# A hybrid attention and expert step on one core: rows turned early, three first units together, last norms scaled last

## The reference, cut to what matters

```
mod = silu(cond) @ w_ada + b_ada          # shift, scale, gate, twice; one set per kind of token
h   = ln_plain(x) * (1 + sc1) + sh1
q,k,v | bq,bk,bv | gates = h @ w_in       # w_in is 1024 x 6656
mix = attention of two kinds, gated;  x = ln_affine(ALPHA*x + g1*(mix @ w_o))
h   = ln_plain(x) * (1 + sc2) + sh2
y   = two of 16 experts per token, weighted and summed
out = ln_affine(ALPHA*x + g2*y, ln2_g, ln2_b)   # mean, variance, gain, bias over 1024
```

## Time and profile before

| what | us |
|---|---|
| median of 3 runs | 1408.13 (1407.26 to 1408.39) |
| the profiled execution's own time | 1407.71 |
| its span, first to last instruction | 1405.9 |
| TensorE busy | 1247.4 (89%) |
| VectorE busy | 972.0 (69%) |
| ScalarE busy | 649.9 (46%) |
| GpSimd busy | 213.6 (15%) |
| mean granted TensorE clock | 0.939 of full speed |

### The profile page before, as it was taken

The page is one execution under the profiler, slowest core; times in us unless marked ns, Lnnn a source line. Parts: engine busy times, 40 slices in busy tenths (PEclk is TensorE's granted clock), DMA queues, the critical chain, the costliest instruction groups (busy, mean ns, idle before and its releaser), DMA issues.

```text
span 1405.9 us, 20426 instructions
## 1 busy us (share of the span) xinstructions
PE 1247.4 (89%) x6656; PEld 1003.2 (71%) x6656; DVE 972.0 (69%) x1750; ACT 649.9 (46%) x1034; POOL 213.6 (15%) x311
## 2 busy tenths in 40 slices
PE   5899999999999899998997999982699999999920
PEld 3577777767888688887876787872588888888820
DVE  4655531656581588788878445897889999999836
ACT  1522222222322487776763222002478888888712
POOL 0022221020223000011111001000111113222101
PEclk9799999999999999999999999985799999999965
DMA  9966764472546768743005433464799999999644
GB/s 350 274 220 200 244 218 173 145 217 75 172 132 203 196 169 213 196 117 103 26 24 181 135 129 141 147 223 195 264 330 365 375 387 386 392 389 383 243 158 75
DMA packets 150274, 301.02 MB, mean 214 GB/s; under 512 B 20349, under 2 KB 31133, under 8 KB 150201
## 3 DMA queue, kind: packets, MB, share of 16 engines
q1 hardware_dynamic: 122280, 232.19, 48.6%
q0 software_dynamic: 22000, 62.64, 14.5%
q10 hardware_dynamic: 5920, 5.24, 1.3%
HBM read 258.69 MB, written 53.90 MB: 222 GB/s over the span
## 4 chain that ended last, share of the span: by engine, by line
PE 76%; DVE 9%; DMA 6%; issue 3%; ACT 2%; SPq 2%; POOL 1%; DVEq 0%; POOLq 0%; ACTq 0%
PE psum_pair L1605 7%; PE psum_pair L1607 7%; PE psum_pair L1606 7%; PE psum_pair L1839 5%; PE psum_pair L1840 5%; PE psum_pair L1841 5%; PE psum_pair L1690 5%; PE psum_pair L1755 4%; PE psum_pair L1757 4%; PE psum_pair L1756 4%; DMA k_bundle<-k_transposed 4%; PE psum_pair L1716 3%; PE psum_pair L1701 3%; PE psum_pair L1854 3%; PE psum_pair L1856 3%
## 5 line engine op out<-in xcount | busy, mean ns | idle before, releaser
L1605 PE MATMUL psum_pair<-w_parts,h_hi 128*128 128x512 f32 x520 | 209.3, 403 | 6.3 <-DVE h_lo L1211 6.3
L1607 PE MATMUL psum_pair<-w_parts,h_lo 128*128 128x512 f32 x520 | 204.9, 394 | 0.0
L1606 PE MATMUL psum_pair<-w_parts,h_hi 128*128 128x512 f32 x520 | 204.6, 393 | 0.0
L1076 DVE TENSOR_TENSOR w_parts<-w_raw,w_parts 128x1024 fp32r<-128x1024 f32 x72 | 83.3, 1219 | 91.2 <-ACT w_parts L819 91.1
L958 ACT ACTIVATE p_unnormed<-psum_pair,minus_max 128x640 f32<-128x640 f32 (+1 forms) x160 | 113.3, 711 | 70.2 <-DVE minus_max L1281 68.9
L1690 PE MATMUL psum_pair<-k_bundle,q_bundle 128*128 128x512 f32 (+1 forms) x576 | 123.3, 342 | 16.1 <-ACT p_unnormed L958 10.2
L1281 DVE TENSOR_REDUCE minus_max<-psum_pair 128x1 f32<-128x640 f32 (+1 forms) x160 | 111.8, 715 | 35.1 <-PE psum_pair L1690 32.9
L1605 PEld LDWEIGHTS psum_pair<-w_parts,h_hi 128*128 128x128 f32 x520 | 98.6, 190 | 37.1 <-issue 18.3
L1690 PEld LDWEIGHTS psum_pair<-k_bundle,q_bundle 128*128 128x128 f32 x576 | 88.5, 194 | 36.9 <-issue 21.5
L1607 PEld LDWEIGHTS psum_pair<-w_parts,h_lo 128*128 128x128 f32 x520 | 98.9, 190 | 21.5
L1606 PEld LDWEIGHTS psum_pair<-w_parts,h_hi 128*128 128x128 f32 x520 | 99.1, 190 | 19.0
(11 more groups left out here) (313 smaller groups left out, 2628.0 us busy)
## 6 DMA issues: line engine op xcount, KB each, us to landing
w_raw<-in_w_gate_up SPq DMA_DIRECT2D x76, 512.0 KB, 8.0
w_raw_c<-in_w_gate_up SPq DMA_DIRECT2D x72, 512.0 KB
w_raw_b<-in_w_down SPq DMA_DIRECT2D x72, 512.0 KB
w_raw<-in_w_in SPq DMA_DIRECT2D x52, 512.0 KB, 8.6
ada_raw<-in_w_ada SPq DMA_DIRECT2D x32, 512.0 KB, 6.8
k_bundle<-k_transposed SPq DMA_DIRECT2D x28, 384.0 KB, 8.7
q_transposed<-turned_staging POOLq DMA_DIRECT2D x40, 256.0 KB, 6.0
ada_raw_early<-in_w_ada SPq DMA_DIRECT2D x16, 512.0 KB, 8.3
```

The costliest lines, as they stand in the source:

```text
L1076: dve.tensor_tensor(w_parts[b % 2][:, 1, c], w_raw[:, c], w_parts[b % 2][:, 0, c].bitcast(F32), ALU.subtract).then_inc(lo_done, 1)
L1605: pe.matmul(bank(n), a_hi, hi, start=first, stop=False)
L1606: pe.matmul(bank(n), a_hi, lo, start=False, stop=False)
L1607: last = pe.matmul(bank(n), a_lo, hi, start=False, stop=end)
```

## The change

Transposes of x: two PSUM users are renumbered so that the 40 transposes stand right after projections 0 and 1 and ahead of turns 0 and 1; even groups are copied out by ScalarE, odd ones by VectorE. The modulation's biases are turned once, by 16 matmuls ahead of projection 0, kept in `mod_b` (with 1 added for the scales), and added by VectorE when the columns come; `turn` for units 0 to 3 has four matmuls and no longer eight. The wait for `mod_done` stands behind the cast of block 0's first chunk. Units 4, 5 and 6 are multiplied together: for each slice k, the three passes of all three tiles. Turns 4 and 5 both stand behind unit 7. The low parts of block 1 are made after `post(5)`.

At the end, the gain comes first: yc = (ya - mean) * gain on VectorE, then the root, and ScalarE's `norm_z` only scales. `square_z` writes its unused product over the x rows. Roots are found for tiles 0 and 1 at once, then 2 and 3, by the general `rsqrt` (eleven instructions), and for tile 4 by `rsqrt_column`. The prompt tile is finished by VectorE with the bias (`ln2_b` is loaded to a free tile) and stored plainly by SyncE; its output is no longer preset. The waits `x7_in` are folded into `x_in`.

```diff
         tr_no, n = {}, 0
-        tr_no[0], tr_no[1] = [0], [1]
-        H_GROUP0 = 2
...
+        TR_BIAS, H_GROUP0 = 0, 1
+        for i in range(N_EARLY):
+            tr_no[i] = [H_GROUP0 + KD + i]
...
@@ SyncE @@
-            for tt in range(NT):
-                dst = t["y_prompt"][0] if tt == PROMPT else t["y_sample"][0, tt * P:(tt + 1) * P]
+            for tt in range(TL):
+                dst = t["y_sample"][0, tt * P:(tt + 1) * P]
                 sp.dma_start(dst, t["ln2_b"][0:1, :].to_broadcast([P, D])).then_inc(out_cleared, 16)
...
+            sp.dma_start(ln2_b, t["ln2_b"][0:1, :].to_broadcast([P, D])).then_inc(lnb_in, 16)
+            sp.wait_ge(zn_finished, 1)
+            sp.dma_start(t["y_prompt"][0], ya[:, PROMPT]).then_inc(prompt_st, 16)
...
@@ ScalarE @@
-            for k in range(KD):
+            for k in range(0, KD, 2):
                 n = H_GROUP0 + k
                 act.wait_ge(tr_ready, n + 1)
                 act.copy(h_mod[:, k], turned(n)[:, 0:NT * P]).then_inc(tr_free[n % 2], 1)
...
-            act.wait_ge(mod_done, 4)
             for c in range(NC_CH):
                 act.wait_ge(raw_in[c], 16)
                 act.copy(w_parts[0][:, 0, c], w_raw[:, c]).then_inc(hi_done, 1)
+                if c == 0:
+                    act.wait_ge(mod_done, 4)
...
-                act.activation(yc[:, tt], ya[:, tt], ACT.Square, bias=zm[:, tt:tt + 1],
+                act.activation(xq[tt], ya[:, tt], ACT.Square, bias=zm[:, tt:tt + 1],
                                accum_out=zq[:, tt:tt + 1]).then_inc(zq_done, 1)
 
             def norm_z(tt):
-                act.wait_ge(zr_done, tt + 1)
-                act.activation(yc[:, tt], ya[:, tt], ACT.Identity, bias=zn[:, tt:tt + 1],
-                               scale=zr[:, tt:tt + 1]).then_inc(zn_done, 1)
...
+                act.wait_ge(zr_done, tt // 2 + 1)
+                act.wait_ge(zg_done, tt + 1)
+                act.activation(ya[:, tt], yc[:, tt], ACT.Copy, scale=zr[:, tt:tt + 1]).then_inc(zn_done, 1)
+
+            square_z(0)
+            square_z(1)
+            norm_z(0)
+            norm_z(1)
+            square_z(2)
+            square_z(3)
+            norm_z(2)
+            norm_z(3)
+            square_z(4)
...
@@ VectorE @@
-                    if ci < 2:
-                        dve.tensor_copy(dst, turned(n)[:, 0:8]).then_inc(tr_free[n % 2], 1)
-                    else:
-                        dve.tensor_scalar(dst, turned(n)[:, 0:8], 1.0, None, ALU.add).then_inc(tr_free[n % 2], 1)
...
+                    dve.tensor_tensor(dst, turned(n)[:, 0:8], bias, ALU.add).then_inc(tr_free[n % 2], 1)
...
+            dve.wait_ge(tr_ready, TR_BIAS + 1)
+            b4 = turned(TR_BIAS)[:, 0:4 * KD].rearrange("p (k c) -> p k c", c=2)
+            dve.tensor_copy(mod_b[:, 0:KD], b4[:, 0:KD]).then_inc(mod_b_done, 1)
+            dve.tensor_scalar(mod_b[:, KD:], b4[:, KD:], 1.0, None, ALU.add).then_inc(tr_free[TR_BIAS % 2], 1)
             for tt in range(NT):
                 dve.tensor_scalar(x5[:, tt], x5[:, tt], mv[:, tt, 0:1], rstd5[:, tt:tt + 1],
                                   ALU.subtract, ALU.mult).then_inc(norm_done, 1)
+            for k in range(1, KD, 2):
+                n = H_GROUP0 + k
+                dve.wait_ge(tr_ready, n + 1)
+                dve.tensor_copy(h_mod[:, k], turned(n)[:, 0:NT * P]).then_inc(tr_free[n % 2], 1)
...
-                if first_of_block(i):
+                if first_of_block(i) and i > N_EARLY:
                     split_lo(units[i][1] + 1)
                 post(i)
+                if i == N_EARLY + 1:
+                    split_lo(1)
...
+                dve.wait_ge(z_done, tt + 1)
+
+            def root_z(c):
+                n = c.stop - c.start
+                dve.wait_ge(zq_done, c.stop)
                 link(dve.tensor_scalar(zv[:, c], zq[:, c], 1.0 / D, EPS, ALU.mult, ALU.add))
-                rsqrt_column(dve, link, zr[:, c], zv[:, c], zt[:], zi[:])
-                dve.tensor_tensor(zn[:, c], zm[:, c], zr[:, c], ALU.mult).then_inc(zr_done, 1)
+                y = zr[:, c]
+                if n == 1:
+                    rsqrt_column(dve, link, y, zv[:, c], zt[:, 0:1], zi[:, 0:1])
+                else:
+                    rsqrt(dve, link, y, zv[:, c], zt[:, 0:n], zi[:, 0:n])
+                    dve.nop().then_inc(zr_done, 1)
 
             def gain_z(tt):
-                dve.wait_ge(zn_done, tt + 1)
-                dve.tensor_tensor(ya[:, tt], yc[:, tt], ln2_g, ALU.mult).then_inc(zg_done, 1)
+                dve.scalar_tensor_tensor(yc[:, tt], ya[:, tt], zm[:, tt:tt + 1], ln2_g, ALU.add, ALU.mult).then_inc(zg_done, 1)
+
+            def finish_z(tt):
+                dve.wait_ge(lnb_in, 16)
+                dve.wait_ge(zg_done, tt + 1)
+                dve.scalar_tensor_tensor(ya[:, tt], yc[:, tt], zr[:, tt:tt + 1], ln2_b, ALU.mult, ALU.add).then_inc(zn_finished, 1)
...
@@ TensorE @@
+            def project_first(group):
+
+                for i in group:
+                    wait_bank(pj_no[i])
+                for kk in range(KD):
+                    hi, lo = w_parts[0][:, 0, kk // 2, kk % 2], w_parts[0][:, 1, kk // 2, kk % 2]
+                    pe.wait_ge(lo_done, kk // 2 + 1)
+                    pe.wait_ge(h_done, kk + 1)
+                    for i in group:
+                        last = times_rows(i, kk, hi, lo)
+                        if kk == KD - 1:
+                            last.then_inc(pj_ready, 1)
...
                         for j in range(4):
-                            out = turned(n)[:, 2 * j:2 * j + 2]
-                            pe.matmul(out, mod_parts[:, ci % 2, j * P:(j + 1) * P], pick_cols[:], start=j == 0, stop=False,
-                                      skip_group_check=True)
-                            last = pe.matmul(out, bias12[:, j * P:(j + 1) * P], pick_rows[:, ci], start=False, stop=True,
-                                             skip_group_check=True)
+                            last = pe.matmul(turned(n)[:, 2 * j:2 * j + 2], mod_parts[:, ci % 2, j * P:(j + 1) * P],
+                                             pick_cols[:], start=True, stop=True)
...
+            for ci in range(N_EARLY):
+                for j in range(4):
+                    c0 = 2 * (4 * ci + j)
+                    last = pe.matmul(turned(TR_BIAS)[:, c0:c0 + 2], bias12[:, j * P:(j + 1) * P], pick_rows[:, ci],
+                                     start=True, stop=True)
+            last.then_inc(tr_ready, 1)
             project(0)
             project(1)
-            turn(0)
-            turn(1)
             pe.wait_ge(norm_done, NT)
...
                 last.then_inc(tr_ready, 1)
+            turn(0)
+            turn(1)
             project(2)
             project(3)
             turn(2)
             turn(3)
-            for i in range(N_EARLY, len(units)):
+            project_first(range(N_EARLY, N_EARLY + 3))
+            for i in range(N_EARLY + 3, len(units)):
                 project(i)
-                if i - 2 >= N_EARLY:
-                    turn(i - 2)
+                if i == N_EARLY + 3:
+                    turn(N_EARLY)
+                turn(i - 2)
...
@@ GpSimd @@
-            pool.wait_ge(out_cleared, 16 * NT)
-            for tt in range(NT):
...
+            pool.wait_ge(out_cleared, 16 * TL)
+            for tt in range(TL):
+                dst = t["y_sample"][0, tt * P:(tt + 1) * P]
+                pool.wait_ge(zn_done, tt + 1)
                 pool.dma_start(dst, ya[:, tt], accum_op=ALU.add).then_inc(out_st, 16)
```

More of the change, by code:

```diff
@@ L296, in hybrid_step @@
         mod_done = sem("mod_columns_done")
+        mod_b_done = sem("mod_bias_done")
         hm_done = sem("h_modulated_done")
@@ L592, in hybrid_step @@
         y_in = [sem(f"pair_rows_in{i}") for i in range(NT)]
-        x7_in = [sem(f"x1_rows_in{i}") for i in range(NT)]
         z_done = sem("z_done")
@@ L601, in hybrid_step @@
         moe_over = sem("moe_over")
-        ln2_g, g2 = rows[:, 0], rows[:, 1:3]
+        lnb_in = sem("ln2_bias_in")
+        zn_finished = sem("z_prompt_finished")
+        prompt_st = sem("prompt_out_stored")
+        ln2_g, g2, ln2_b = rows[:, 0], rows[:, 1:3], yo[:]
         xq = [rows[:, 3], rows[:, 4], x1_b[:, 0], x1_b[:, 1], x1_c[:]]
@@ L1560, in _ @@
-            dve.wait_ge(s7_in, 48)
-            for tt in range(NT + 2):
-                if tt < NT:
-                    combine(tt)
-                if tt >= 2:
-                    gain_z(tt - 2)
-                if 1 <= tt <= NT:
-                    root_z(tt - 1)
+                y = zr[:, c]
[4 more added lines that the diff above has]
+                    dve.nop().then_inc(zr_done, 1)
@@ L1569, in _ @@
+            gain_z(1)
+            root_z(slice(0, 2))
+            combine(2)
+            gain_z(2)
+            combine(3)
+            gain_z(3)
+            root_z(slice(2, 4))
+            combine(4)
+            gain_z(4)
+            root_z(slice(4, 5))
+            finish_z(4)
```

54 lines of the change are left out of this document (24 added, 30 removed).

## The result

| | us |
|---|---|
| before, same chip | 1407.70 (1407.07 to 1408.39) |
| after | 1383.45 (1382.62 to 1384.65) |
| ratio | 0.983 (95% interval 0.9814 to 0.9846) |
| predicted | 1388, range 1384 to 1394 |

The kernel is 24.2 us faster. The profiled execution of after took 1383.63 us, its span is 1381.8.

A forecast was written before the change was run, and what follows sets the result against it. TensorE was taken to wait at the start on its modulation columns, then VectorE; VectorE bounds the end. Start 14.9 plus end 4.7 is 19.6 us off 1407.71, 1388.1, adjusted to 1388.5, stated as 1388; range 1384 to 1394.

The forecast's parts named there:

- The start: From the first loads through joint units 4 to 6: predicted to end 14.9 us earlier, floor 9.4, ceiling 17.2.
- The biases: 16 bias matmuls before projection 0: 5.0 us, up to 8 at low clock, free because TensorE has nothing before 13.01.
- The second copier: VectorE copying transposes out of PSUM beside ScalarE: predicted to hardly help, with the transposes taking 6.2 us.
- The three steps from there to the first product: From complete modulation columns to the first joint-unit product: times 38.8, 40.1 and 41.6 us.
- The gain is the order: At the transposes: the gain was credited to their starting at 23.4, not 29.19, rather than to the second copier.
- The joint units: Units 4 to 6: 72 matmuls without starving, ten at low clock, 18.7 us, ending at 60.3 against 75.14.
- split_lo(1): Block 1's low parts between post 5 and post 6 on VectorE, 4.62 us: predicted to cost nothing.
- The end: Last stage: 4.7 us gained, between 0 and 6; VectorE 34.25, store landing taken as 4.2, then 3.9 unchanged.
- Early clock: Rival at the start: bias matmuls lower TensorE's clock early, start gain becomes 9.4, total 1393.6; chance 0.12.
- Hidden end: Rival in the last stage: prompt store or tile 3's accumulation ends as late as before, total 1392.8; chance 0.09.
- Start given back: Rival before the attention: a later block's weights set the pace, all 14.9 us lost, total 1403.0; chance 0.05.
- Low clock into later blocks: Slower rival: low clock continues past the joint units; slower if it lasts some 44 us from 41.6; chance 0.02.

The follow-up runs named there:

- after_again: The changed kernel run once more, unchanged: 1384.42 us, ratio 0.9827 to the kernel before.
- front_only: The new start with the old last stage, the fold of the x waits kept: 1391.76 us, ratio 0.9887 to the kernel before.
- sums_on_gpsimd: Changed kernel with GpSimd adding the two experts' rows of the third and fifth tile in the last stage: 1388.08 us, ratio 0.9855 to the kernel before.
- prompt_by_gpsimd: Changed kernel with the prompt tile's plain store issued from GpSimd's queue instead of SyncE's: 1386.61 us, ratio 0.9844 to the kernel before.
- gained_tables: Changed kernel with the second layer's head-norm gain multiplied into the rope tables, one VectorE pass less per rotated unit: 1378.89 us, ratio 0.9792 to the kernel before.
- bias_in_turns: Changed kernel with biases added inside turns 0 to 3 again (eight matmuls each), early bias matmuls kept: 1393.34 us in one execution.
- turns_first: Changed kernel with turns 0 and 1 ahead of the transposes again: 1383.79 us in one execution.
- before_again: The kernel before the change, unchanged, traced a second time: 1406.41 us.
- tail_only: The old start with the new last stage: 1398.11 us, ratio 0.9935 to the kernel before.
- cast_late: Changed kernel with the wait for the modulation columns ahead of the first cast again: 1385.12 us in one execution.
- one_copier: Changed kernel with all eight groups of transposes copied by ScalarE: 1384.59 us in one execution.
- units_apart: Changed kernel with units 4, 5 and 6 one after the other again, block 1's low parts ahead of post 4: 1389.95 us, ratio 0.9888 to the kernel before.

## Why the prediction was off

**The start: right in its sum, in part by luck.** More executions than one pair bear on it. Scores of the old start are at 466.9, 468.1 and 467.7, mean 467.6; of the new start (after, after_again, front_only, sums_on_gpsimd, prompt_by_gpsimd) at 451.9 to 453.3, mean 452.3. It is worth 15.3 us; I said 14.9. But at the turn in front of block 1 the same executions are 16.4 us ahead (87.6 on average in the three old starts, 71.3 in the five new ones), and 1.1 us of this is lost again in block 7, where the clock fell in three of the five new ones and in none of the old. So the edits gave 1.5 us more than the sum had, and a fall of the clock that the sum didn't have took most of it back. By steps:

- The biases cost nothing, as said, but their price was too low: 6.95 us, not 5.0. In after they end at 11.98 and the first projection begins at 12.68. In gained_tables and bias_in_turns they began at 6.32 and 6.19 and ran into it: it starts at 13.20 and 13.07 without a wait, and projection 1 still ends with its weights, at 23.55 and 22.91. The cover of 13 us is used up.
- Transposes from 23.14 to 29.3, with 6.2 us as predicted, from VectorE's copy at 0.82 us (I took 0.86). The second copier does little, as I said.
- A turn is four matmuls of one kind and takes 0.97 to 1.06 us, not 1.25. My 0.31 us a piece came from rows in which pick and bias alternate; the turns without them go at 0.24 to 0.27. The columns were complete at 37.4, not 38.8. The three steps from there to the first product took 2.8 us, as predicted.
- "The gain is the order" is refuted by turns_first (0.3 us at the first product) and bias_in_turns (8.6, of which at least 7.4 are the pairing). The clock's part was a matter of chance as well: I wrote that the turns let it fall after 3.7 us and that 2.5 us might not. In before_again, tail_only and bias_in_turns it fell 1.9 to 2.7 us after the turns began, and in four of the ten executions with short turns it fell 1.7 to 2.5 us after the first pair began, near its end. The sum hid this, because I had taken order and pairing together in one time line.
- The joint units ran without a wait, ten matmuls at the low clock, as in the sum (in after_again the low clock lasted 1.8 us longer, to 46.6).
- `split_lo(1)` ran from 61.70 to 66.3 and no TensorE wait followed.
- The start is not given back before the scores, but the profiled execution of after, 16.57 ahead near block 1, lost 1.7 of it in block 7 to a clock drop. after_again had a slower beginning (its turns 4 and 5 at 65.53, not 64.07) and no drop in block 7, and came to the same 451.9.

**The end: the step that failed.** "The plain store ... I take 4.2" and "the 3.9 us from the last landing to the span's end stay" were both too high. VectorE's part was right to 0.1 us: 34.3 from the first sum to the issue, for 34.35. Behind it I counted 8.1 us; ten executions show 4.9 to 6.9. The landing I took from a plain load and the rest from GpSimd's queue. Neither row was about a store by SyncE, and I had given the rest no bounds at all. The estimate of 3.2 us by the Trainium skill's page "DMA: Bandwidth & Descriptors" (section "Anatomy of one DMA"), which I had set aside for the 5.3 of a store that accumulates, is nearer than my 4.2: the median of the ten landings is 3.1. The page fits it to transfers issued by GpSimd, whose one plain store here landed after 2.9; it gives no scatter, and SyncE's ranged from 2.6 to 4.3. Over the nine executions that share the new last stage in full the end is 39.1 to 41.0, mean 39.9, against 47.2: worth 7.3 us, not 4.7. These 2.6 us are the largest part of the 4.6 by which the forecast was off.

**The rest.** 15.3 and 7.3 are 22.6 of the 24.2 us. The stretch between the marks ranges from 888.6 to 895.6 in the fourteen profiles, with no order by kernel (before 891.8 and 889.2; after 889.0 and 895.6), and moves in part with waits of 1.5 to 6.6 us for keys being loaded back (cast_late has 4.2 us of them and the short 888.8). Its mean is 889.9 over the three executions with the old start and 891 over the other eleven. The 2.8 us between the first two profiles are therefore from execution to execution. What of the remaining 1.6 us of the medians is this, and what is the change, stays open.

**The rivals.** Early clock: no, 1.00 from 5 to 36 us in after; though in gained_tables, prompt_by_gpsimd, one_copier and cast_late it was low during projections 2 and 3, which took 1.1 to 1.4 us longer there. Hidden end: no, tail_only alone ends 7.8 us earlier behind the first sum. Start given back: no. Low clock into later blocks: no, PEclk is 1.00 in after from 46 to 270 us, and the fall in block 7 lasts some 3.5 us. The range's lower end named "no low clock and a faster store"; the faster store alone went beyond it.

## What to carry to other kernels

Price the last store from issue to the end of the span, not to its landing, and from a row of the same queue: the part behind the landing was 2.5 us for SyncE and 3.9 to 5.1 for GpSimd here. Where several edits feed one time line, put a price on each alone before naming the one that pays: here sixteen tiny matmuls moved into an empty stretch were worth at least 7.4 of 9.9 us, and the reordering nothing that a run shows. A second engine for an elementwise stage pays only if both engines keep their speed side by side, and VectorE and GpSimd did not. Before calling a difference between two traces the work of an edit, see how far two traces of one kernel differ at the same place: here by 6.6 us between marks that no edit touches.

## What the runs showed of the hardware that I had not expected

- Where the granted clock falls around the turns changes from execution to execution. With paired turns it fell 1.9 to 3.7 us after a first pair began (four executions); with short ones it fell near the end of the first pair in four executions and kept 1.00 there in six. That the small matmuls are the cause isn't shown: 16 of the bias kind, 6.95 us long, kept 1.00 in all eleven executions that have them at the start. Projections 2 and 3, the same 32 matmuls, took 3.71 to 4.19 us at 1.00 (five executions; in a sixth, sums_on_gpsimd, they also waited for weights) and 5.02 to 5.34 where the clock had fallen (five, with bias_in_turns).
- The same stop of 2.6 to 2.7 us in block 7 was followed by a granted clock of 0.50 for some 3.5 us in seven executions (after, front_only, units_apart, one_copier, bias_in_turns, cast_late, prompt_by_gpsimd), and by 1.00 in six (before, before_again, tail_only, turns_first, after_again, sums_on_gpsimd). The three with the old start are all among the six; whether the new start makes the fall likelier stays open.
- A plain store of 512 KB by SyncE landed after 2.6 to 2.8 us in five executions and after 3.4 to 4.3 in the other five, less than any plain load of that size in the earlier trace rows in all but the longest.
- A sum of 128x1024 elements took 2.35 us on GpSimd, and 3.04 where it began beside a VectorE pass. VectorE's takes 1.22 us alone and took 3.36 when it began 0.08 us behind GpSimd's.
